# A decoder layer on one core: the first feed-forward layer as seven block products of sums of blocks

## The chip, the cores and the metric

The kernel runs on one core of one Trainium2 chip. The metric is the device time of one launch in microseconds (us); lower is better. Three runs of the kernel before gave 1168.57, 1169.19 and 1167.16 us, median 1168.57 us.

## The reference, cut to what matters

One decoder layer for 512 prompt tokens and 64 sample tokens (8 sequences of 8), 576 columns in all, width 1024: a mixer of gated linear attention and latent attention, a cross-attention into 256 memory tokens, and the feed-forward sublayer, which is all that the change touches:

```python
D_MODEL = 1024
D_FF = 4 * D_MODEL

def ffn(h, lp):
    u = jnp.maximum(h @ lp['w_ff1'], 0)
    return (u * u) @ lp['w_ff2']

x = x + ffn(rms_norm(x, lp['g_ff']), lp)
```

Everything is float32 in the reference. The first layer takes 1024 features to 4096, the second takes 4096 back to 1024.

## The kernel before, in words

**Layout.** Activations lie transposed: features on the 128 partitions, the 576 tokens as columns. `xT` holds x in KD = 8 tiles of 128 features. A matmul has a 128x128 block of weights as the stationary side and 288 columns (HALF, half of the tokens, index c) as the moving side; it adds into one of eight PSUM banks. Weights arrive in 512 KB tiles (128 output features by 1024 input features, or by 1024 hidden features for the second layer) in a ring of SLOTS = 8 buffers, `ring`. SP issues the loads in order, each when the slot's last contents have been split.

**Three terms.** Each float32 operand is split into a high part (rounded to the fp32r type) and a low part (what is left). A product is high x high, high x low, low x high (TERMS), so three matmuls for each block and half. The split weights lie in `wr`, those of h = x times the gain g_ff in `hr`, those of the squared hidden values in `ur`. The division by the norm is not done on h: the second layer's result is multiplied by `r_ff` = 1/(mean square + eps), which is enough because u is squared and relu keeps the factor.

**The stretch before.** The cross-attention's output projection (`xo`, matmuls L1372) makes 8 output tiles, each of two halves of 12 matmuls. Banks turn, and the last half (7, 1) lies in bank 0. DVE adds each half to `xT` (L2377, `add_half`) and frees its bank; behind each pair of additions it does the low part of the tile of h before it (L2430, `low_part`), for tiles 5 and 6 the low part of a weight tile too (L2440). ACT makes the high part (L1848) and the square of x (L1851); POOL adds the squares up in `acc` (L2820, `add_squares`).

**The feed-forward.** 64 weight tiles in two halves of the hidden features. In each half 16 tiles of the first layer (`split_tile`, L1388): 48 matmuls, 8 blocks x 3 terms x 2 halves of the columns, into two banks, and then 8 output tiles of the second layer, two weight tiles each. These are loops on every engine (`Fori`), each pass with 8 tiles. For each weight tile DVE makes the high part (L2597) and the low part (L2599); `wr` has SPLITS = 2 places. For each hidden tile ACT does the relu of both halves (L1860, L1863), the square (L1868) and its high part (L1870), and DVE the low part (L2609). For each output tile DVE multiplies a half by `r_ff` (L2628) and adds it to `xT` (L2631). After the first 16 hidden tiles PE sums `acc` over the partitions (L1404, key `ms_ff`, banks 4 and 5), and DVE adds eps (L2644) and takes the reciprocal (L2645), once for each half. The next matmuls, of output tiles 0 and 1, use banks 0 to 3. POOL has no work in the feed-forward after the squares. At the end PE turns `xT` back into rows (L1423).

**Order and waits.** Each engine runs its own queue in order. `filled`/`full` and `freed`/`reopen` are the semaphores of a bank: PE fills it and the reader waits, the reader frees it and PE waits before it starts a new sum there. `make_plan` gives each sum its bank. `w_high` and `w_split` count the split weights, `h_high` and `h_low` the parts of h, `u_high` and `u_low` the parts of the hidden values.

## Time and profile before

| | before |
|---|---|
| median of three runs | 1168.57 us |
| the profiled execution, its own time | 1168.92 us |
| its span, first to last instruction | 1167.1 us |
| PE busy (matmul) | 1132.3 us, 97% |
| PEld, weight loads | 1025.2 us, 88% |
| DVE busy | 649.9 us, 56% |
| ACT busy | 380.8 us, 33% |
| POOL busy | 313.0 us, 27% |
| mean granted TensorE clock | 0.992 of full speed |
| moved by DMA | 114.21 MB, mean 98 GB/s |

The span is the time that the trace covers; the execution's own time is 1.8 us longer. Busy is the share of the span in which an engine has an instruction in work; matmuls are pipelined, so the mean of one (296 ns) is longer than the pace at which they follow each other. The pace is the busy time of a group by the number in it.

### The profile page before, as it was taken

To read this page: it belongs to the slowest core of one execution; us is meant where nothing else is said; L and a number is where in the kernel's file an instruction comes from. 1 tells how busy PE (TensorE), PEld (TensorE's weight loads), DVE (VectorE), ACT (ScalarE), POOL (GpSimd) and SP (SyncE) were. 2 spreads that over 40 slices of the span, in tenths; PEclk is the share of its full clock that TensorE was granted. 3 is DMA by queue.
4 is the path that set the end of the run, shared out by engine and by line. 5 is a ranking of instruction groups with operands and counts; after the bars stand their busy time and mean duration, and the time that the engine had idled before them with its cause. 6 is when DMAs were issued, how large, how long until landed. Compare 5 with 4: busy or idle time off the path is not lost.

```text
span 1167.1 us, 22516 instructions
## 1 busy us (share of the span) xinstructions
PE 1132.3 (97%) x8288; PEld 1025.2 (88%) x8288; DVE 649.9 (56%) x1100; ACT 380.8 (33%) x872; POOL 313.0 (27%) x180
## 2 busy tenths in 40 slices
PE   7999999999999999999989989999999999999997
PEld 4799897577899999999869956999999999999996
DVE  0649653677566667766657566534354444444443
ACT  4331114455555445545502263423300013330001
POOL 0116224450277676876612201200000000000000
PEclk9999998999999999999999999999999999999999
DMA  9422102041454444454115240322223222222102
GB/s 339 175 91 91 59 1 64 1 133 68 122 158 120 122 127 122 135 143 126 40 41 212 91 162 20 109 91 73 90 73 91 75 87 86 77 90 73 55 0 81
DMA packets 61603, 114.21 MB, mean 98 GB/s; under 512 B 6577, under 2 KB 41554, under 8 KB 61458
## 3 DMA queue, kind: packets, MB, share of 16 engines
q1 hardware_dynamic: 60946, 111.33, 30.0%
q0 software_dynamic: 576, 1.84, 0.5%
q8 instruction: 45, 0.74, 0.3%
q14 instruction: 36, 0.29, 0.1%
HBM read 107.90 MB, written 5.25 MB: 97 GB/s over the span
## 4 chain that ended last, share of the span: by engine, by line
PE 88%; DVE 5%; POOL 2%; ACT 1%; DMA 1%; issue 1%; SPq 1%; POOLq 0%; DVEq 0%; ACTq 0%
PE bank L1388 35%; PE bank L1161 5%; PE bank L1230 5%; PE bank L1163 5%; PE bank L1162 5%; PE bank L811 4%; PE bank L829 4%; PE bank L773 3%; PE bank L1117 2%; POOL stat L2805 2%; PE bank L1372 2%; PE bank L991 2%; PE bank L1071 2%; PE bank L1169 1%; PE bank L977 1%; PE bank L1091 1%
## 5 line engine op out<-in xcount | busy, mean ns | idle before, releaser
L1388 PE MATMUL bank<-hr,wr 128*128 128x288 f32 x1536 | 205.2, 296 | 1.3 <-DVEq L2379 1.3
L1388 PEld LDWEIGHTS bank<-hr,wr 128*128 128x128 f32 x1536 | 204.9, 189 | 1.5 <-issue 1.5
L1388 PE MATMUL bank<-ur,wr 128*128 128x288 f32 x1536 | 205.3, 296 | 0.0
L1388 PEld LDWEIGHTS bank<-ur,wr 128*128 128x128 f32 x1536 | 205.0, 189 | 0.1
L2805 POOL TENSOR_TENSOR stat<-stat,cst 128x32 f32<-128x32 f32 x32 | 175.8, 5493 | 2.5
L2597 DVE CAST wr<-ring 128x1024 fp32r<-128x1024 f32 x62 | 43.0, 694 | 209.1 <-PE bank L1388 208.7
L1161 PE MATMUL bank<-wq_high,c_parts 128*128 128x288 f32 x512 | 156.8, 306 | 1.0 <-ACT mixT L1693 1.0
L1163 PE MATMUL bank<-wq_low,c_parts 128*128 128x288 f32 x512 | 151.7, 296 | 0.0
L1162 PE MATMUL bank<-wq_high,c_parts 128*128 128x288 f32 x512 | 150.3, 294 | 0.0
L2262 DVE TENSOR_REDUCE stat<-hT 128x8 f32<-128x512 f32 x128 | 86.7, 682 | 62.9 <-ACT hT L1711 61.0
L1161 PEld LDWEIGHTS bank<-wq_high,c_parts 128*128 128x128 f32 x512 | 96.1, 188 | 7.6 <-issue 7.1
L1162 PEld LDWEIGHTS bank<-wq_high,c_parts 128*128 128x128 f32 x512 | 96.4, 188 | 0.0
L1163 PEld LDWEIGHTS bank<-wq_low,c_parts 128*128 128x128 f32 x512 | 96.3, 188 | 0.0
L1860 ACT ACTIVATE hT<-bank 128x288 f32<-128x288 f32 x32 | 13.2, 412 | 236.2 <-PE bank L1388 236.2
L1711 ACT ACTIVATE hT<-bank 128x512 f32<-128x512 f32 x128 | 77.8, 608 | 0.3 <-DVE stat L2262 0.3
L2599 DVE TENSOR_TENSOR wr<-ring,wr 128x1024 fp32r<-128x1024 f32 x62 | 76.0, 1226 | 2.1
L1703 ACT COPY arena<-bank 128x64 f32<-128x64 f32 x128 | 27.2, 212 | 122.6 <-PE bank L1163 83.9
L2803 POOL TENSOR_TENSOR stat<-stat,cst 128x32 f32<-128x32 f32 x32 | 17.8, 557 | 82.4 <-DVE stat L2262 82.3
L811 PE MATMUL bank<-h_high,wz 128*128 128x288 f32 x176 | 38.3, 299 | 0.2 <-DVE ring_low L1948 0.2
L1877 ACT COPY hT<-bank 128x512 f32<-128x512 f32 (+1 forms) x5 | 2.9, 585 | 106.8 <-PE bank L1423 103.6
L811 PE MATMUL bank<-h_high,ring_low 128*128 128x288 f32 x176 | 37.5, 295 | 0.0
L811 PE MATMUL bank<-h_low,wz 128*128 128x288 f32 x176 | 37.5, 294 | 0.0
(421 smaller groups left out, 1964.4 us busy)
## 6 DMA issues: line engine op xcount, KB each, us to landing
ring<-in_ring_w_dram SPq DMA_DIRECT2D x106, 512.0 KB, 3.6
arena<-in_page_rows_dram SPq DMA_DIRECT2D x128, 144.0 KB, 2.2
hT<-in_ckv_t_dram SPq DMA_DIRECT2D x64, 128.0 KB, 2.1
arena<-in_ckv_t_dram SPq DMA_DIRECT2D x64, 128.0 KB, 2.1
arena<-in_mk_t_dram SPq DMA_DIRECT2D x8, 512.0 KB, 5.6
arena<-in_cache_mv_dram SPq DMA_DIRECT2D x8, 512.0 KB, 8.3
mixT<-in_x_dram SPq DMA_DIRECT2D x1, 2048.0 KB, 13.1
out_dram<-hT SPq DMA_DIRECT2D x4, 512.0 KB, 3.2
```

What stands on the lines that cost most here:

```text
L811: ins = mm(outs[c][:, 0:HALF], w_part(ew, tile)[:, k * P:(k + 1) * P], h_part(eh, k)[:, c * HALF:(c + 1) * HALF], start=(k == 0 and n == 0 ...
L829: ins = mm(outs[t][0:m, 0:width], h_part(eh, k)[:, c0:c0 + m], w_part(ew, tile)[:, kk * width:(kk + 1) * width], start=(k == 0 and n == 0) ...
L1161: mm(o[:, 0:WQ - QH], c_parts[:, n % 2, 0, e, k, :], high, start=(k == 0), stop=False)
L1162: mm(o[:, 0:WQ - QH], c_parts[:, n % 2, 1, e, k, :], high, start=False, stop=False)
L1163: ins = mm(o[:, 0:WQ - QH], c_parts[:, n % 2, 0, e, k, :], low, start=False, stop=(k == KC - 1))
L1230: ins = mm(outs[c][:, 0:HALF], w[:, k * P:(k + 1) * P], src[ex][:, k, c * HALF:(c + 1) * HALF], start=(k == 0 and n == 0), stop=(k == KD - ...
L1388: ins = mm(outs[c][:, 0:HALF], w[:, ew, k, :], src[:, ex, k0 + k, c * HALF:(c + 1) * HALF], start=(start and k == 0 and n == 0), stop=(sto ...
L1711: A(sqs[:, j % 2, :].rearrange("p (e c) -> p e c", e=2), o[:, :, keys_at:keys_at + WQ - 2 * QH], ACT.Square).then_inc(S("kr_free"), 1)
L2262: V.tensor_reduce(stat[:, 64 + 32 * g + 8 * (j % 4):72 + 32 * g + 8 * (j % 4)], sqs[:, j % 2, :].rearrange("p (h c) -> p h c", h=MH), AX.X ...
L2597: V.tensor_copy(wr[:, j % SPLITS, 0, :], src).then_inc(S("w_high"), 1)
L2599: V.tensor_tensor(wr[:, j % SPLITS, 1, :], src, wr[:, j % SPLITS, 0, :], ALU.subtract).then_inc(S("w_split"), 1)
L2805: G.tensor_tensor(r, r, power.broadcast_to([P, 32]), ALU.pow).then_inc(S("r_pg"), 1)
```

## The change

The first layer is computed by groups of two weight tiles, which are a 2 x 2 matrix of blocks: A11 and A12 are the upper and the lower 512 input features of the first tile (its 128 output features), A21 and A22 those of the second. h is a 2 x 2 matrix too: the upper or lower 512 features by the left or right 288 columns. Eight block products (of 12 matmuls: 4 blocks of 128 x 3 terms) are replaced by seven, of sums of blocks (Winograd's form of Strassen's product). The first group, g = 0, is left plain (`plain`), since h is then still arriving; 15 groups remain.

- **Weights.** POOL makes S1 = A21 + A22, S2 = S1 - A11, S3 = A11 - A21 and S4 = S2 - A12 (`weight_sum`, 128x512 each). The seven operands, of 128x512, are split by ACT (high part, `high_of`) and DVE (low part, `low_of`) into `wr`, which has OPERANDS = 7 places. All 16 second-layer operands of a quarter go the same way.
- **h.** DVE makes the sums of h for the four blocks k = 0 to 3 (`column_sums`, four instructions of 128x288 each); ACT and POOL (DVE for the fourth) split them, 128x1152 each.
- **Products.** `group`: A11, S2, S1, A22, A12, S3, S4, each 12 matmuls into one bank (`product`); A12, S3 and S4 are added onto the banks of A11, S2 and S1 after these have been read. The groups use banks 0 to 3 and 4 to 7 in turn.
- **Outputs of a group.** ACT copies A11 and S1 out, DVE makes the four hidden halves by five additions or subtractions of 128x288 (`outputs_of`); then relu, square and split as before.
- **Quarters.** Four quarters of the hidden features in place of two halves: 8 first-layer tiles, then 8 output tiles of one weight tile each (`second`), so `xT` gets four additions for each half tile in place of two. In the first quarter `ms_ff` stands after 8 hidden tiles, in banks 2 and 3.
- **No loops.** The feed-forward is written out on every engine.

The diff, cut to its core:

```diff
+M_ORDER = ("A11", "S2", "S1", "A22", "A12", "S3", "S4")
+BANK_OF = {"A11": 0, "A12": 0, "S2": 1, "S3": 1, "S1": 2, "S4": 2, "A22": 3}
...
+        if q == 0:
             for c in range(2):
+                fill(("ms_ff", c), 2 + c)
+        for j in range(KD):
             for c in range(2):
+                fill(("f2", q, j, c), (2 * j + c) % 8)
...
+            def product(name, g, start=True):
+
+                m = FIRST["g", g] + M_ORDER.index(name)
+                o = reopen(pe, (name, g))
+                pe.wait_ge(S("w_split"), split_number(m))
+                for k in range(HK):
+                    for n, (ew, ex) in enumerate(TERMS):
+                        ins = mm(o[:, 0:HALF], wr[:, m % OPERANDS, ew, k * P:(k + 1) * P], hr[:, X_OF[name], ex, k, :],
+                                 start=(start and k == 0 and n == 0), stop=(k == HK - 1 and n == 2),
+                                 skip_group_check=True)
+                filled(ins, (name, g))
...
+                pe.wait_ge(S("u_low"), KD * (q + 1) - 2)
+                second(q, 0, 0, KD - 2)
+                second(q, 1, 0, KD - 2)
+                pe.wait_ge(S("u_low"), KD * (q + 1))
+                second(q, 0, KD - 2, KD)
+                second(q, 1, KD - 2, KD)
...
+            act.wait_ge(S("ff_step"), 4 * HK)
+            for x in ("S2", "S1", "S3"):
+                nc.scalar.copy(hr[:, X_OF[x], 0, :, :], hf[:, X_OF[x], 1, :, :]).then_inc(S("h_high"), 1)
...
+            def high_group(g):
+
+                m, k = FIRST["g", g] + OPERANDS, 2 * g % KD
+                o = full(act, ("A11", g))
+                freed(nc.scalar.copy(m1[:, g % 2, :], o[:, 0:HALF]), ("A11", g))
+                high_of(m)
+                high_of(m + 1)
+                o = full(act, ("S1", g))
+                if g > 1:
+                    read(act, ("A22", g - 1))
+                freed(nc.scalar.copy(m5, o[:, 0:HALF]), ("S1", g))
+                high_of(m + 2)
+                high_of(m + 3)
+                o = full(act, ("A12", g))
+                act.wait_ge(S("u_low"), 2 * g)
+                freed(A(u_sb[:, 0, 0, :], o[:, 0:HALF], ACT.Relu), ("A12", g))
+                high_of(m + 4)
+                high_of(m + 5)
+                read(act, ("A22", g))
+                A(u_sb[:, 1, :, :], u_sb[:, 1, :, :], ACT.Relu).then_inc(S("u"), 1)
+                act.wait_ge(S("u"), 4 * g - 1)
+                A(u_sb[:, 1, :, :], u_sb[:, 1, :, :], ACT.Square).then_inc(S("u"), 1)
...
             def low_part_behind(j):
                 if j:
                     low_part(j - 1)
                 if j in (2, 4):
                     late_low(LATE_XO + 1 + j // 2)
+                if j > HK:
+                    column_sums(j - HK - 1)
                 if j in (5, 6):
+                    low_of(FIRST_OP + 2 * (j - 5))
+                    low_of(FIRST_OP + 2 * (j - 5) + 1)
...
+            def outputs_of(g):
+
+                m = FIRST["g", g] + OPERANDS
+                m1_g = m1[:, g % 2, :]
+                low_of(m)
+                o = full(dve, ("S2", g))
+                read(dve, ("A11", g))
+                freed(V.tensor_tensor(u2, m1_g, o[:, 0:HALF], ALU.add), ("S2", g))
+                for n in range(1, 5):
+                    low_of(m + n)
+                o = full(dve, ("S3", g))
+                read(dve, ("S2", g))
+                freed(V.tensor_tensor(m1_g, m1_g, o[:, 0:HALF], ALU.add), ("S3", g))
...
+                V.tensor_tensor(u_sb[:, 1, 1, :], m1_g, m5, ALU.subtract)
+                o = full(dve, ("A22", g))
+                freed(V.tensor_tensor(u_sb[:, 1, 0, :], m1_g, o[:, 0:HALF], ALU.add), ("A22", g))
+                low_of(m + 5)
+                o = full(dve, ("S4", g))
+                freed(V.tensor_tensor(u_sb[:, 0, 1, :], u2, o[:, 0:HALF], ALU.subtract), ("S4", g))
+                hidden_low(2 * g + 1, 1, 2 * g + 1)
+                hidden_low(2 * g, 0, 2 * g + 2)
+                low_of(m + 6)
...
+            def weight_sum(g, name, a, b, op, behind=None):
+
+                n = SUMS.index(name)
+                if behind is not None:
+                    pool.wait_ge(S("acc"), sum_number(g, SUMS.index(behind)))
+                if g > 1:
+                    pool.wait_ge(S("w_split"), split_number(FIRST["g", g - 1] + M_ORDER.index(name)))
+                G.tensor_tensor(sums_sb[:, n, :], a, b, op).then_inc(S("acc"), 1)
```

**What moves on DVE ahead of the feed-forward.** The two rows L2377 below are the last additions to `xT`, of tile 7; the second frees bank 0, the first bank of the feed-forward. Before:

```order
L2377 TENSOR_TENSOR xT<-xT,bank6 128x288 [waits x_cross,bank_full6]
L2430 SCALAR_TENSOR_TENSOR hr<-xT,gn,hr 128x576 [waits x_cross,h_high]
L2440 TENSOR_TENSOR wr<-ring,wr 128x1024 [waits w_high]
L2377 TENSOR_TENSOR xT<-xT,bank6 128x288 [waits bank_full7]
L2377 TENSOR_TENSOR xT<-xT,bank0 128x288 [waits x_cross,bank_full0]
L2430 SCALAR_TENSOR_TENSOR hr<-xT,gn,hr 128x576 [waits x_cross,h_high]
L2430 SCALAR_TENSOR_TENSOR hr<-xT,gn,hr 128x576 [waits h_high]
```

Now (L2571 is the addition, L2624 the low part of h, L2639 to L2647 `column_sums`, L2630 `low_of`):

```order
L2571 TENSOR_TENSOR xT<-xT,bank6 128x288 [waits x_cross,bank_full6]
L2624 SCALAR_TENSOR_TENSOR hr<-xT,gn,hr 128x2x288 [waits x_cross,h_high]
L2639 SCALAR_TENSOR_TENSOR hf<-xT,gn,arena 128x288 [waits h_high]
L2642 SCALAR_TENSOR_TENSOR hf<-xT,gn,hf 128x288 [waits ff_step]
L2644 SCALAR_TENSOR_TENSOR hf<-xT,gn,arena 128x288
L2647 SCALAR_TENSOR_TENSOR arena<-xT,gn,hf 128x288 [waits ff_step]
L2630 TENSOR_TENSOR wr<-ring,wr 128x512 [waits w_high] x2
L2571 TENSOR_TENSOR xT<-xT,bank6 128x288 [waits bank_full7]
L2571 TENSOR_TENSOR xT<-xT,bank0 128x288 [waits x_cross,bank_full0]
```

Four instructions stand between two pairs of additions that were not there; this happens behind tiles 5 and 6, and twice more behind tile 7.

**What moves on PE around `ms_ff`.** Before, the sums over the partitions go to banks 4 and 5 (L1404), and the output tiles behind them start in banks 0 to 3. Now, at the end of the first quarter (L1482 `product`, L1534 `ms_ff`, L1516 `second`):

```order
L1482 MATMUL bank6<-hr,wr 128x288 x11
L1534 MATMUL bank2<-rstd,cst 128x288 [waits bank_free2,acc]
L1534 MATMUL bank2<-rstd,cst 128x288 [waits bank_free3]
L1516 MATMUL bank0<-ur,wr 128x288 [waits bank_free1,w_split,bank_free0,u_low]
L1516 MATMUL bank0<-ur,wr 128x288 x23
L1516 MATMUL bank0<-ur,wr 128x288 [waits w_split]
L1516 MATMUL bank0<-ur,wr 128x288 x11
L1516 MATMUL bank2<-ur,wr 128x288 [waits w_split,bank_free3,bank_free2]
```

The names give the even bank of a pair. Only 36 matmuls stand between the sums and the next use of banks 2 and 3.

**What DVE has in its queue there.** The end of group 3 and what frees banks 2 and 3 (L2835 to L2849 `outputs_of`, L2814 `hidden_low`, L2860 and L2861 eps and reciprocal):

```order
L2846 TENSOR_TENSOR hT<-hT,bank6 128x288 [waits bank_full7]
L2630 TENSOR_TENSOR wr<-ring,wr 128x512 [waits w_high]
L2849 TENSOR_TENSOR hT<-hT,bank6 128x288 [waits bank_full6]
L2814 TENSOR_TENSOR ur<-hT,ur 128x576 [waits u_high] x2
L2630 TENSOR_TENSOR wr<-ring,wr 128x512 [waits w_high]
L2860 TENSOR_SCALAR bank2<-bank2 128x288 [waits bank_full2]
L2861 RECIPROCAL rstd<-bank2 128x288 [waits dve_step]
L2860 TENSOR_SCALAR bank2<-bank2 128x288 [waits bank_full3]
L2861 RECIPROCAL rstd<-bank2 128x288 [waits dve_step]
```

The reciprocals stand behind the group's two low parts of the hidden values, which wait for ACT.

## Rows read from the trace of the kernel before

**Rows 1.** The page: busy time; then the chain that ended last

```profile
PE 1132.3 (97%) x8288; PEld 1025.2 (88%) x8288; DVE 649.9 (56%) x1100; ACT 380.8 (33%) x872; POOL 313.0 (27%) x180
...
PE bank L1388 35%; PE bank L1161 5%; PE bank L1230 5%; PE bank L1163 5%; PE bank L1162 5%; PE bank L811 4%; PE bank L829 4%; PE bank L773 3%; PE bank L1117 2%; POOL stat L2805 2%; PE bank L1372 2%; PE bank L991 2%; PE bank L1071 2%; PE bank L1169 1%; PE bank L977 1%; PE bank L1091 1%
```

**Rows 2.** Groups by line and form, feed-forward: busy us, mean ns | idle before

```profile
L1388 PE MATMUL bank<-ur,wr 128*128 128x288 f32 x1536 | 205.3, 296 | 0.0
L1388 PE MATMUL bank<-hr,wr 128*128 128x288 f32 x1536 | 205.2, 296 | 1.3 <-DVEq L2379 1.3
L2609 DVE TENSOR_TENSOR ur<-hT,ur 128x576 f32 x32 | 24.3, 758 | 13.4 <-ACT ur L1870 13.4
L1868 ACT ACTIVATE hT<-hT 128x576 f32<-128x576 f32 x32 | 22.0, 687 | 3.0
L1870 ACT CAST ur<-hT 128x576 f32 x32 | 21.6, 675 | 3.9
L2628 DVE TENSOR_TENSOR bank<-bank,rstd 128x288 f32<-128x288 f32 x32 | 14.7, 459 | 8.9 <-PE bank L1388 8.9
L1860 ACT ACTIVATE hT<-bank 128x288 f32<-128x288 f32 x32 | 13.2, 412 | 236.2 <-PE bank L1388 236.2
```

**Rows 3.** Groups of other stages, for sizes that the feed-forward lacks

```profile
L1665 ACT CAST c_parts<-arena 128x512 fp32r<-128x512 f32 x32 | 19.9, 621 | 1.3 <-DMA arena<-in_page_rows_dram 1.3
L1746 ACT CAST mix_high<-mixT 128x1152 fp32r<-128x1152 f32 x3 | 3.4, 1171 | 0.0
L2502 DVE TENSOR_TENSOR hT<-hT,stat 128x512 f32<-128x512 f32 x4 | 2.8, 692 | 0.1
L2370 DVE TENSOR_TENSOR mix_low<-mixT,mix_high 128x1152 fp32r<-128x1152 f32 x3 | 4.0, 1352 | 0.2 <-DVE mix_low L2421 0.2
L2781 POOL TENSOR_TENSOR wq_low<-w_kvb,wq_high 128x512 fp32r<-128x512 f32 x2 | 2.5, 1266 | 0.2
L2712 POOL TENSOR_TENSOR mixT<-arena,mixT 128x1152 f32<-128x1152 f32 x1 | 3.1, 3143 | 10.0 <-ACT mixT L1512 10.0
```

**Rows 4.** Timeline of DVE into the feed-forward: start us, us

```profile
735.17 1.04 DVE L2377 TENSOR_TENSOR xT<-xT,bank 128x288 f32<-128x288 f32 x2
736.36 0.82 DVE L2430 SCALAR_TENSOR_TENSOR hr<-xT,gn,hr 128x576 fp32r<-128x576 f32 x1
737.10 1.22 DVE L2440 TENSOR_TENSOR wr<-ring,wr 128x1024 fp32r<-128x1024 f32 x1
738.23 1.05 DVE L2377 TENSOR_TENSOR xT<-xT,bank 128x288 f32<-128x288 f32 x2
739.43 1.25 DVE L2430 SCALAR_TENSOR_TENSOR hr<-xT,gn,hr 128x576 fp32r<-128x576 f32 x1
740.60 1.21 DVE L2440 TENSOR_TENSOR wr<-ring,wr 128x1024 fp32r<-128x1024 f32 x1
741.74 1.04 DVE L2377 TENSOR_TENSOR xT<-xT,bank 128x288 f32<-128x288 f32 x2
```

**Rows 5.** Timeline of PE there: last matmuls of `xo`, first of the feed-forward

```profile
741.24 0.29 PE L1372 MATMUL bank<-xo_high,ring_low 128*128 128x288 f32 x1
741.37 0.29 PE L1372 MATMUL bank<-xo_high,wo_high 128*128 128x288 f32 x1
741.50 0.29 PE L1372 MATMUL bank<-xo_low,wo_high 128*128 128x288 f32 x1
741.63 0.29 PE L1372 MATMUL bank<-xo_high,ring_low 128*128 128x288 f32 x1
743.18 2.08 PE L1388 MATMUL bank<-hr,wr 128*128 128x288 f32 x14 [1.26 <-DVEq L2379]
```

**Rows 6.** Timeline of POOL in the same stretch

```profile
738.63 1.44 POOL L2820 TENSOR_TENSOR rstd<-rstd,hT 128x576 f32<-128x576 f32 x1 [2.09 <-ACT hT L1851]
740.74 2.33 POOL L2820 TENSOR_TENSOR rstd<-rstd,hT 128x576 f32<-128x576 f32 x1 [0.68 <-ACT hT L1851]
```

**Rows 7.** Timeline of DVE around `ms_ff`

```profile
848.77 0.46 DVE L2644 TENSOR_SCALAR bank<-bank 128x288 f32<-128x288 f32 x1
...
851.61 1.96 DVE L2645 RECIPROCAL rstd<-bank 128x288 f32<-128x288 f32 x1
```

**Rows 8.** PE in two stretches: length, busy us (matmuls), granted clock, DMA share, GB/s

```profile
700.00:717.00 17.00, 15.57 (x86) 0.97 0.00 1
1160.00:1167.10 7.10, 0.38 (x4) 0.86 0.68 245
```

More of the change, by code:

```diff
@@ L446, in build @@
         acc = r_ff = rstd[:, :]
-        ACC_FF = 2 * (KD - 1) + XH
         pcxT = view(arena, 17920, XH, 2, TP)
@@ L1375, in _, with plain @@
                     filled(ins, ("xo", j, c))
[L1379 to L1384 removed]
+            def plain(j):
+                outs = [reopen(pe, ("plain", j, c)) for c in range(2)]
+                for k in range(KD):
+                    m = FIRST["g", 0] + 2 * j + k // HK
+                    if k % HK == 0:
+                        pe.wait_ge(S("w_split"), split_number(m))
+                    if j == 0:
@@ new lines, in group @@
+            def group(g):
+                product("A11", g)
+                if g == 1:
+                    pe.wait_ge(S("acc"), COLUMN_LOW[0])
+                product("S2", g)
+                if g == 1:
+                    pe.wait_ge(S("acc"), COLUMN_LOW[1])
+                product("S1", g)
+                if g == 1:
+                    pe.wait_ge(S("h_low"), KD + 1)
+                product("A22", g)
+                product("A12", g, start=False)
+                if g == 1:
+                    pe.wait_ge(S("acc"), COLUMN_LOW[2])
+                product("S3", g, start=False)
+                product("S4", g, start=False)
@@ L1401, in _ @@
+            for q in range(QUARTERS):
+                for g in range(GROUPS * q, GROUPS * (q + 1)):
+                    if g == 0:
+                        plain(0)
+                        plain(1)
+                    else:
+                        group(g)
+                if q == 0:
                     pe.wait_ge(S("acc"), ACC_FF)
@@ L2633, in _, with hidden_low @@
-            for _ in range(2):
-                dve.nop().then_inc(S("u_low"), 1)
             add_to_x("xo", "x_cross", in_turn, low_part_behind)
             low_part(KD - 1)
-            for half in range(2):
-                with dve.Fori(0, KF // 16) as i:
-                    hidden(half, i)
-                if half == 0:
-                    full(dve, ("ms_ff", 0))
+            column_sums(HK - 1)
+            def hidden_low(n, which, number):
+                dve.wait_ge(S("u_high"), number)
+                V.tensor_tensor(ur[:, 1, n % KD, :], u_sb[:, which, :, :].rearrange("p c n -> p (c n)"),
+                                ur[:, 0, n % KD, :], ALU.subtract).then_inc(S("u_low"), 1)
@@ L2642, in _ @@
+            for q in range(QUARTERS):
+                for g in range(max(1, GROUPS * q), GROUPS * (q + 1)):
+                    outputs_of(g)
+                if q == 0:
                     for c in range(2):
-                        o = bank[PLAN[("ms_ff", c)][0]]
+                        o = full(dve, ("ms_ff", c))
                         link(V.tensor_scalar(o[:, 0:HALF], o[:, 0:HALF], EPS, None, ALU.add))
```

366 lines of the change are left out of this document (231 added, 135 removed).

## The prediction

> **What bounds the kernel now.** I read the page first: PE is busy for 97% of the span, and the chain that ended last is PE nearly everywhere, 35% of it on L1388, the feed-forward [rows 1]. Then the groups of that stage: the two layers take 205.2 and 205.3 us for 1536 matmuls each, 133.6 ns per matmul, with 1.3 us of idle time in all [rows 2]. So a matmul left out there is worth 133.6 ns, as long as nobody makes PE wait. DVE, ACT and POOL wait for PE there now; the question is how near they come to it when each gets more work and PE less. For that I took durations of the same shapes from other stages [rows 3], and looked at two places in time: the way into the feed-forward [rows 4, 5, 6] and the reciprocals [rows 7].
>
> **Matmuls.** Two weight tiles cost 96 matmuls, 12.83 us. As a group they cost 7 x 12 = 84, 11.22 us. 15 groups save 180 matmuls: 180 x 0.1336 = **24.05 us**. The new products put twelve matmuls in a row into one bank. The `xo` matmuls of before do just that, and they start 0.13 us apart [rows 5], so I add nothing.
>
> For the pace the Trainium skill ("TensorE: Matmul & The Clock Gate", section "Wait — 56ns, not 53.3ns?") gives N / 2.4 GHz plus about 2.5 ns for bf16, an estimate of 122.5 ns at N = 288. By that the saving would be 22.1 us and the forecast 2 us higher; the rows have 133.6 ns, and they decide.
>
> **Into the feed-forward (a loss).** `plain(0)` starts in bank 0 and must wait for the last addition of `xo`, as before: PE's last `xo` matmul starts at 741.63, its next at 743.18, released by DVE [rows 5]. DVE is the engine behind time here: the pairs of additions start at 735.17, 738.23 and 741.74 [rows 4], while PE makes a pair in 24 matmuls, 3.2 us. Now two `column_sums` stand ahead of the last pair. Each has four instructions of 128x288; I take the 0.46 us of L2628 [rows 2] for each, which lie between about 0.37 apart back to back and 0.6 with a wait for the one before: 1.7 us for four, 3.4 us for two. POOL's additions stand in the way besides: one of them took 2.33 us in place of 1.44 beside a DVE instruction with two inputs in SBUF [rows 6], and L2430 took 1.25 in place of 0.82 beside another [rows 4]. I add 1.0 us, so the last pair ends 4.4 us later and PE starts at 747.6.
>
> Then group 1 needs all of the split sums of h. From the last addition (742.8 + 4.4 = 747.2): DVE does two low parts (0.8 each) and two `column_sums` (1.7 each), with one wait for POOL 6.0 us: 753.2. ACT's first 128x1152 cast 1.17 [rows 3]: 754.4. POOL then does the first low part, 3.14 at that size, and S1 and S2 of the weights, 1.27 each [rows 3]: 760.1. ACT stands behind them in its queue: casts of the two sums 1.2, two relus, a square and a cast of hidden tile 0, 2.3, two casts 1.2, two relus 0.7, the cast of the fourth sum of h 1.17: 766.7. DVE makes its low part in 1.35 [rows 3], but POOL may be in its third 3.14 us instruction: between 768.1 and 771.2, I take 769.6. There product A22 can start; four products of 1.60 us are left of the group: 776.0. Without any wait group 1 would have ended at 743.18 + 180 x 0.1336 = 767.2. The loss is **8.8 us**, between 6 and 11.7.
>
> **`ms_ff` (a loss).** Before, the output tiles in banks 0 to 3 (12.8 us) covered eps and the reciprocals, 848.77 to 853.57, 4.8 us [rows 7]. Now the next use of banks 2 and 3 comes 36 matmuls (4.8 us) and the two sums (0.5 us) after the group's end. DVE reaches the reciprocals only after the low parts of both hidden tiles, for which ACT does a relu, a square and a cast (0.69 + 0.69 + 0.68) and then 0.41 + 0.69 + 0.68 [rows 2]; with gaps and DVE's own 0.76 and 0.69 that is 5.9 us after the group's end, and with the reciprocals 10.7. PE waits 10.7 - 5.3 = 5.4; with a collision now and then **5.5 us**, between 4 and 7.
>
> **In the groups (a loss).** Work per group, against PE's 11.22 us: ACT seven casts of 128x512 at 0.62, four instructions of 128x288 at 0.41, five of 128x576 at 0.68, 9.4 us; DVE seven subtractions at 0.69, five at 0.46, two at 0.76, 8.7 us; POOL four at 1.27, 5.1 us [rows 2, 3]. Each fits alone. But they wait for each other. From ACT's copy of A11: copies, casts and the relu up to the cast of A12's weights 4.3 us, DVE's low part of it 0.7, three additions 1.4, ACT's three and three more 4.3, the last cast 0.6: a ring of 11.3 us, as long as PE's group. Its slack is what PE grants before it needs the banks of A11 and S2 again, about 1.2 us, once a quarter. And POOL's sums stop DVE: DVE's instructions with two SBUF inputs and POOL's together are 4.8 + 0.5 + 1.5 + 5.1 = 11.9 us in a group. With two POOL instructions on the ring it is 12.9 us, 1.7 above PE's. POOL has ring tiles to sum only in the first two groups of a quarter (the next quarter's tiles are not loaded yet), so I take half of it, 0.95 us, for the 8 middle groups, less 1.2 us of slack in three quarters: 7.6 - 3.6 = **4.0 us**, between 0 and 14 x 1.7 = 24.
>
> **Costed at nothing.** The splits of second-layer weights: 2 x 0.62 on ACT and 2 x 0.69 on DVE in 6.4 us of PE. The doubled additions to `xT`: four of 0.46 for each output tile, with the splits 3.2 of 6.4 us; if that cover went, each tile would cost what exceeds 6.4. The wait for the last hidden tiles of a quarter: `second` puts 72 matmuls, 9.6 us, ahead of it, and the low parts come 5.2 us after the group's end. The loads: the same 64 tiles of 512 KB, one in 5.6 us, some 94 GB/s; the kernel already moves more than that in its tail [rows 8]. The end: the last output tile has the same four DVE instructions behind it. The loops: none showed idle time on PE.
>
> **Sum.** -24.05 + 8.8 + 5.5 + 4.0 = -5.75 us. Against the execution's own 1168.92 that is 1163.2, and it stands 0.35 above the median: 1168.57 - 5.75 = **1162.8 us**.
>
> **The rivals.**
> *The covers hold.* DVE wins its collisions with POOL, and the ring of ACT and DVE stays within PE's group. For it: the durations have some overlap (the second of a pair starts before the first has ended), which shortens the ring. Against it: at the two ends the order of the queue alone makes the loss. -24.05 + 6 + 4.5 + 0.5 = -13: 1155.5 us.
>
> *The ring binds every group (slower).* Place: ACT's copy of A11 and DVE's `u2` addition, for which A12 and S3 wait. Price: 12.9 - 11.22 = 1.68 us in each of 14 groups, 23.5 us in place of 4: 1182.3 us. It needs POOL to be let in ahead of DVE each time, in every group. For it: in the rows a DVE instruction that met a POOL instruction did not share, it waited [rows 4, 6]. Against it: POOL has no sums to make in half of the groups. It decides from 24.05 - 14.3 = 9.75 us of waits, 0.70 us per group; at half its price the kernel takes 1171.
>
> The Trainium skill ("SBUF — State Buffer", section "Who interferes with whom") says that whichever of DVE and GpSimd issues first has the shared ports for its whole instruction and the other blocks. By that, 2.33 for 1.44 us agrees, and it speaks against this change: every weight sum can hold up DVE for its full length.
>
> *The clock falls.* PE now idles for some 6 us before the feed-forward and 5.5 us at `ms_ff`. In the trace the granted clock was 0.97 in 17 us with 1.4 us of idle time, and 0.86 in the tail, where PE has next to nothing to do [rows 8]. If it fell to 1.2 GHz for as long as PE had waited, the matmuls behind would cost up to 2.9 us more at `ms_ff`, and up to 0.5 at the start, where group 1 waits anyway for A22: 1166.2 us, at the very edge of what counts as no change, where I count it. The Trainium skill ("TensorE: Matmul & The Clock Gate", Part 1) has it that idleness throttles the array to half its clock until it has been busy for a while; at the small gaps of this trace the clock hardly showed it.
>
> **How the numbers follow.** 0.2%, 2.3 us, is about what a measurement of this kernel can tell from no change. The forecast has 0.48, the covers 0.14, the clock 0.15, the binding ring 0.23. Forecast and covers are faster by over 0.2%: 0.62. The clock is within: 0.15. The ring is slower: 0.23. The range goes down a little below the covers, to 1154, and up to 1176, which takes in the ring at up to two thirds of its price and leaves out about 0.15 above.
>
> **What would show it.** The first-layer matmuls should be 1356 in number and the second's 1536, at 133 ns each when nothing waits. PE should show a gap of 5 to 7 us before the first, a wait of some 2 to 5 us in group 1 whose releaser is the low part of the fourth sum of h, and one of 5 to 6 us at bank 2 released by the reciprocal. DVE and POOL instructions should be longer than alone in the first two groups of a quarter, and PE's waits in later groups should lie at A12 and S3. It would be wrong if PE went through the sums without the gap at `ms_ff`, or if groups of the last quarters took more than 12 us each, which is the ring.

## The result, and the profile after

The changed kernel takes 1171.62 us (median of 22 runs, 1167.13 to 1174.56), the kernel before 1168.36 us in 22 runs on the same chips. The ratio is 1.0024, with a 95% interval of 1.0013 to 1.0035: slower, by some 2.8 us, about as much as a measurement can tell (0.2%). The forecast was 1162.8. The time lies within its range, and the direction is wrong. The profiled execution took 1168.68 us, its span 1166.9; it is one of the quicker ones, so the trace is compared by stretches and not by its whole time.

The page, busy time:

```profile
PE 1113.3 (95%) x8108; PEld 1006.6 (86%) x8108; DVE 743.1 (64%) x1303; ACT 489.2 (42%) x1066; POOL 410.0 (35%) x243
```

PE is busy for 19 us less than in [rows 1], so the matmuls did go. The span did not shrink with them. The groups of the feed-forward on PE (line, form, count, busy us and mean ns, idle time before and what ended it) show where part of it went:

```profile
L1516 PE MATMUL bank<-ur,wr 128*128 128x288 f32 x1536 | 207.1, 297 | 5.8 <-issue 5.8
L1482 PE MATMUL bank<-hr,wr 128*128 128x288 f32 x1260 | 172.0, 298 | 8.0 <-DVE hr L2823 6.9 <-ACT hT L2029 0.9 <-DVE wr L2630 0.3
L1470 PE MATMUL bank<-hr,wr 128*128 128x288 f32 x96 | 15.1, 325 | 6.8 <-DVEq L2573 6.8
```

1260 and 96 are the 1356 first-layer matmuls. The idle time is 20.6 us against 1.3 in [rows 2], and the busy time is longer than the count explains: 15.1 us for 96 matmuls is 157 ns each, not 133.6. The timeline of PE (start, us, then the row, then the idle time before it) puts each in its place:

```profile
746.15 15.09 PE L1470 MATMUL bank<-hr,wr 128*128 128x288 f32 x96 [6.80 <-DVEq L2573]
761.08 1.76 PE L1482 MATMUL bank<-hr,wr 128*128 128x288 f32 x12
763.11 3.52 PE L1482 MATMUL bank<-hr,wr 128*128 128x288 f32 x24 [0.28 <-DVE wr L2630]
773.53 31.08 PE L1482 MATMUL bank<-hr,wr 128*128 128x288 f32 x216 [6.90 <-DVE hr L2823]
...
816.19 47.91 PE L1516 MATMUL bank<-ur,wr 128*128 128x288 f32 x348 [5.82 <-issue]
863.94 28.95 PE L1482 MATMUL bank<-hr,wr 128*128 128x288 f32 x216
893.18 16.27 PE L1482 MATMUL bank<-hr,wr 128*128 128x288 f32 x120 [0.29 <-ACT hT L2029]
909.30 51.35 PE L1516 MATMUL bank<-ur,wr 128*128 128x288 f32 x384
```

Three gaps, all in the first quarter: before the feed-forward, at A22 of group 1, at `ms_ff`. The quarters behind have one wait of 0.28 or 0.29 us each. And the same 216 matmuls take 31.08 us behind the second gap and 28.95 in the next quarter. The stretches of PE tell why (length, busy us and count of PE and PEld, DVE, ACT, POOL, then the granted clock, the DMA share and GB/s):

```profile
746.15:752.00 5.85, 5.85 (x28) 5.85 (x29) 5.74 (x9) 1.27 (x2) 1.41 (x1) 0.60 0.23 86
752.00:765.00 13.00, 12.72 (x95) 12.45 (x94) 5.94 (x6) 8.86 (x15) 10.91 (x6) 1.00 0.00 0
773.53:780.00 6.47, 6.47 (x33) 6.47 (x34) 6.39 (x8) 1.74 (x4) 3.85 (x3) 0.64 0.51 162
816.19:822.00 5.81, 5.81 (x34) 5.81 (x35) 0.00 (x0) 0.00 (x0) 0.00 (x0) 0.75 0.01 3
822.00:830.00 8.00, 8.00 (x62) 8.00 (x61) 5.76 (x12) 2.29 (x4) 0.00 (x0) 1.00 0.19 68
```

Behind each gap the granted clock is 0.60, 0.64 and 0.75, means between the two levels of 1.2 GHz (0.5) and 2.4 GHz (1.00), and then it is 1.00 again. In 746.15 to 752.00 PE never rested and did 28 matmuls, 209 ns each.

The account runs from the start of the last `xo` matmul (741.63 before, 739.05 after) to the first turning matmul at the end (1155.82, 1155.59). I call this **the stretch**: what lies ahead of it is the same code, and the last `xo` matmul started anywhere from 738.9 to 745.4 us in the traces of the changed kernel and its variants. It is 414.19 us before and 416.54 after, 2.35 more. By the starts in the timeline, against 133.6 ns a matmul:

- matmuls left out, 180 x 0.1336: -24.05;
- last `xo` matmul to the first of the feed-forward, 7.10 in place of 1.55: +5.55;
- plain group, 14.93 for 12.83: +2.10, clock;
- group 1 to the end of the quarter's first layer, 761.08 to 804.45 for 252 matmuls (33.67 us): +9.70, of it 7.18 waits, 2.06 slow matmuls behind A22 (30.92 us for 216, 28.86 at full pace), and 0.46 in the matmuls just before the two waits, whose ends lie behind the pace;
- the second layer of the first quarter with `ms_ff`, 805.21 to 863.94, 58.73 us for 384 matmuls that later take 51.19 (909.30 to 960.49): +7.54, of it 5.82 the wait, 1.36 slow matmuls behind it (47.75 us for 348, 46.39 at the later pace), and the rest before it;
- the later quarters, 45.36 for 336 matmuls (44.89): three times 0.47, +1.41.

The sum is +2.25, beside the measured 2.35 for these two traces.

What makes the second gap shows in DVE's timeline ahead of A22, one instruction a line, POOL's beside it, and ACT's cast of the fourth sum of h:

```profile
760.46 2.51 DVE L2630 TENSOR_TENSOR wr<-hT,wr 128x512 fp32r<-128x512 f32 x1 [3.21 <-ACT wr L1983]
762.89 1.77 DVE L2630 TENSOR_TENSOR wr<-hT,wr 128x512 fp32r<-128x512 f32 x1
764.59 1.84 DVE L2814 TENSOR_TENSOR ur<-hT,ur 128x576 fp32r<-128x576 f32 x1
766.35 3.12 DVE L2630 TENSOR_TENSOR wr<-ring,wr 128x512 fp32r<-128x512 f32 x1
769.40 1.75 DVE L2630 TENSOR_TENSOR wr<-ring,wr 128x512 fp32r<-128x512 f32 x1
771.07 2.41 DVE L2823 TENSOR_TENSOR hr<-arena,hr 128x1152 fp32r<-128x1152 f32 x1
```

```profile
759.73 2.68 POOL L3052 TENSOR_TENSOR hr<-hf,hr 128x1152 fp32r<-128x1152 f32 x1
762.37 1.75 POOL L3062 TENSOR_TENSOR hT<-ring 128x512 f32<-128x512 f32 x1
764.08 1.74 POOL L3062 TENSOR_TENSOR hT<-hT,ring 128x512 f32<-128x512 f32 x1
765.78 3.15 POOL L3052 TENSOR_TENSOR hr<-hf,hr 128x1152 fp32r<-128x1152 f32 x1
768.89 1.70 POOL L3062 TENSOR_TENSOR hT<-ring 128x512 f32<-128x512 f32 x1
770.67 1.59 POOL L3062 TENSOR_TENSOR hT<-hT,ring 128x512 f32<-128x512 f32 x1
```

```profile
764.58 1.15 ACT L2016 CAST hr<-arena 128x1152 fp32r<-128x1152 f32 x1
```

DVE has six instructions from 760.46 to 773.48 and POOL six from 759.73 to 772.26. Alone DVE's six would take 4 x 0.69 + 0.76 + 1.35 = 4.9 us [rows 2, 3]; they took 13.0, with no idle time in between. The two engines take turns, one instruction each: five of POOL's end at 762.4, 764.1, 765.8, 768.9 and 770.6, and 0.55 to 0.6 us behind each of them one of DVE's ends; the sixth of DVE's, the longer one, ends 1.2 us behind POOL's last. It is so in the rest of the trace: of 171 low parts of weights on DVE from 740 us on, 32 took 1.4 us or more, and within each of the 32 lies the end of exactly one POOL instruction. ACT's cast of the fourth sum of h ended at 765.73, and DVE's low part of it at 773.48.

### The profile page after: what moved, and what is told of

It is laid out like the page before. It is cut to its first block, busy times and chain, and to the rows that moved or that the text cites. A ratio compares the mean times of both kernels' runs of the same rounds, so it can differ in the third digit from the quotient of the medians.

```text
span 1166.9 us, 22259 instructions
## 1 busy us (share of the span) xinstructions
PE 1113.3 (95%) x8108; PEld 1006.6 (86%) x8108; DVE 743.1 (64%) x1303; ACT 489.2 (42%) x1066; POOL 410.0 (35%) x243
## 4 chain that ended last, share of the span: by engine, by line
PE 76%; DVE 9%; POOL 5%; ACT 4%; issue 3%; DMA 1%; POOLq 0%; SPq 0%; DVEq 0%; ACTq 0%
PE bank L1516 17%; PE bank L1482 9%; PE bank L891 6%; PE bank L1310 5%; PE bank L1241 4%; PE bank L909 4%; POOL stat L3025 4%; PE bank L1243 4%; PE bank L1242 4%; PE bank L1197 3%; PE bank L853 2%; DVE wr L2630 2%; PE bank L1071 2%; PE bank L1151 2%; PE bank L1452 1%
## 5 line engine op out<-in xcount | busy, mean ns | idle before, releaser
L1516 PE MATMUL bank<-ur,wr 128*128 128x288 f32 x1536 | 207.1, 297 | 5.8 <-issue 5.8
L1516 PEld LDWEIGHTS bank<-ur,wr 128*128 128x128 f32 x1536 | 206.3, 190 | 6.1 <-issue 6.0
L1482 PE MATMUL bank<-hr,wr 128*128 128x288 f32 x1260 | 172.0, 298 | 8.0 <-DVE hr L2823 6.9
L1482 PEld LDWEIGHTS bank<-hr,wr 128*128 128x128 f32 x1260 | 170.4, 190 | 9.3 <-DVE hr L2823 7.1
L1983 ACT CAST wr<-ring 128x512 fp32r<-128x512 f32 x113 | 66.8, 619 | 127.6 <-PE bank L1516 117.4
L3062 POOL TENSOR_TENSOR hT<-ring 128x512 f32<-128x512 f32 x30 | 44.1, 1472 | 209.7 <-DVE wr L2630 157.7
L2630 DVE TENSOR_TENSOR wr<-ring,wr 128x512 fp32r<-128x512 f32 x113 | 97.0, 887 | 4.8 <-ACT wr L1983 4.5
L2868 DVE TENSOR_TENSOR bank<-bank,rstd 128x288 f32<-128x288 f32 x64 | 29.6, 462 | 100.7 <-PE bank L1516 100.7
L3062 POOL TENSOR_TENSOR hT<-hT,ring 128x512 f32<-128x512 f32 x30 | 47.4, 1581 | 25.5 <-DVE wr L2630 24.3
L1983 ACT CAST wr<-hT 128x512 fp32r<-128x512 f32 x60 | 36.5, 620 | 47.4 <-PE bank L1516 31.6
L2630 DVE TENSOR_TENSOR wr<-hT,wr 128x512 fp32r<-128x512 f32 x60 | 50.5, 867 | 3.2 <-ACT wr L1983 3.2
L2814 DVE TENSOR_TENSOR ur<-hT,ur 128x576 fp32r<-128x576 f32 x32 | 27.8, 869 | 33.3 <-ACT ur L2048 18.2
```

The costliest lines, as they stand in the source:

```text
L1482: ins = mm(o[:, 0:HALF], wr[:, m % OPERANDS, ew, k * P:(k + 1) * P], hr[:, X_OF[name], ex, k, :], start=(start and k == 0 and n == 0), sto ...
L1516: ins = mm(bank[PLAN["f2", q, j, c][0]][:, 0:HALF], wr[:, m % OPERANDS, ew, k % HK * P:(k % HK + 1) * P], ur[:, eu, k, c * HALF:(c + 1) * ...
L1983: nc.scalar.copy(wr[:, m % OPERANDS, 0, :], source(m)).then_inc(S("w_high"), 1)
L2630: V.tensor_tensor(wr[:, m % OPERANDS, 1, :], source(m), wr[:, m % OPERANDS, 0, :], ALU.subtract).then_inc(S("w_split"), 1)
L3062: G.tensor_tensor(sums_sb[:, n, :], a, b, op).then_inc(S("acc"), 1)
```

## The experiments

Each kernel is the changed one with the edit shown. The stretch is read from its profiled execution, the ratio is against the kernel before.

**1. Other banks for `ms_ff`.**

```diff
-                fill(("ms_ff", c), 2 + c)
+                fill(("ms_ff", c), 4 + c)
```

> The two sums of ms_ff go to banks 4 and 5, as before the change, in place of 2 and 3; all else is the changed kernel (1171.6 us median, ratio 1.0024 to the kernel before; its profiled execution 1168.68). Gaps theory: the wait of 5.8 us ahead of output tile 1 goes, because banks 4 and 5 are wanted only 12.8 us after the sums, and with it the stretch at a granted clock of 0.66 to 0.76 behind it, worth about 1.9 us: 7 to 8 us less, ratio to the kernel before 0.996 to 0.998. Rival (DVE is behind in any case, so the wait only moves to output tile 2): 0 to 2 us less.

1164.7 us, ratio 0.9966 (0.9951 to 0.9981). The stretch is 409.10, 7.44 less than the change's, where the account has 7.54 for this gap. PE's groups in it:

```profile
L1516 PE MATMUL bank<-ur,wr 128*128 128x288 f32 x1536 | 205.6, 296 | 0.0
L1482 PE MATMUL bank<-hr,wr 128*128 128x288 f32 x1260 | 171.9, 297 | 8.3 <-DVE hr L2823 6.9 <-ACT hT L2029 0.9 <-DVE wr L2630 0.5
```

As expected, the wait is gone, and with it 1.5 us of busy time in the same 1536 matmuls. One wait of 5.82 us cost 7.4. The page puts this wait down to "issue" and names no releaser; that it is the banks of `ms_ff` follows from this run, and from the second reciprocal, which ends at 816.09, 0.1 us before PE goes on. The other two gaps stayed as they were.

**2. The fourth sum's low part ahead in DVE's queue.** ACT's cast of it comes first, DVE does it ahead of weight operands 10 and 11 and of the first hidden tile. On DVE:

```diff
-            hidden_low(0, 0, 1)
+            dve.wait_ge(S("h_high"), 2 * KD + 4)
+            V.tensor_tensor(hr[:, 3, 1, :, :], t4, hr[:, 3, 0, :, :], ALU.subtract).then_inc(S("h_low"), 1)
             low_of(10)
             low_of(11)
-            dve.wait_ge(S("h_high"), 2 * KD + 4)
-            V.tensor_tensor(hr[:, 3, 1, :, :], t4, hr[:, 3, 0, :, :], ALU.subtract).then_inc(S("h_low"), 1)
+            hidden_low(0, 0, 1)
```

> Around groups 0 and 1, ACT casts the fourth sum of h as soon as the plain tiles are read, ahead of the square and cast of hidden tile 0, and DVE makes its low part ahead of the low parts of two weight operands and of hidden tile 0. Order theory: the wait of 6.9 us ahead of product A22 of group 1 falls to 1 to 3 us and the slow clock behind it goes too, worth about 2: 5 to 7 us less than the changed kernel. Lock rival (DVE is held up by POOL's three low parts and four sums at that place whatever the order, since both are served in turn): the low part of the weights of A22 or A12 comes as late as the sum did, and the gain is under 2 us.

1170.59 us, ratio 1.0015 (0.9998 to 1.0031), stretch 416.17, 0.4 less than the change's. PE's timeline in group 1:

```profile
766.31 3.52 PE L1482 MATMUL bank<-hr,wr 128*128 128x288 f32 x24 [0.46 <-DVE wr L2632]
773.40 4.95 PE L1482 MATMUL bank<-hr,wr 128*128 128x288 f32 x24 [3.57 <-DVE wr L2632]
780.70 27.35 PE L1482 MATMUL bank<-hr,wr 128*128 128x288 f32 x192 [2.35 <-issue]
```

Waits of 0.28 and 6.90 became three, 6.4 together. The order in the queue only chooses which product waits; DVE's time is what is short. The theory of the order, by which 5 to 7 us were to go, falls.

**3. PE kept busy in the three gaps**, with matmuls whose result nobody reads (50, 50 and 42).

```diff
+                for i in range(n):
...
+                    mm(o[:, 0:HALF], w, x, start=True, stop=True)
...
+                    keep_busy(50, ("xo", 7, 0))
```

> 142 matmuls that compute nothing are put into PE's three long waits (50 before group 0, 50 ahead of product A22 of group 1, 42 ahead of output tile 1), into banks that are free. The waits themselves stay. Clock theory: the granted clock stays at 1.00 in and after the gaps; group 0 takes 12.8 us in place of 14.9, but product A22 starts when it did, since it waits for the low part of the fourth sum; what is gained is the slow stretch behind A22 and behind ms_ff, 2.5 + 1.9 = 4.4 us less than the changed kernel. Rival (the matmuls behind the gaps are slow for a reason of their own, such as the loads of instructions or the fresh banks): the same stretches stay slow, 0 us less or a little more.

1169.63 us, ratio 1.0005 (0.9992 to 1.0019), stretch 415.24, 1.3 less than the change's. PE's timeline:

```profile
752.52 13.01 PE L1481 MATMUL bank<-hr,wr 128*128 128x288 f32 x96 [0.26 <-DVEq L2588]
769.44 4.96 PE L1493 MATMUL bank<-hr,wr 128*128 128x288 f32 x24 [2.32 <-DVE wr L2645]
```

The filler gave the plain group its full clock, 13.01 us for 15.09, and the second layer 205.8 for 207.1. So the slow matmuls come from the gaps. But 4.4 us were expected, and 1.3 came. The plain group's 2.1 us came back as a wait of 2.32 for DVE, behind which 24 matmuls again took 4.96 us (some 3.4 at full pace). PE was early at a place where DVE sets the time, so the clock lost in the plain group was mostly cover, and only the clock behind A22 and behind `ms_ff` can be on the path. The filler also ran over the event that it covered: A22 started 35.6 us after the last `xo` matmul, in the change 34.5. From A22 to the end of the stretch 2.4 us were gained, of the 3.4 that the account has there as slow matmuls: at A12 of group 2 PE now waited 0.79 us for ACT (L2044), where it had not before.

**4. Weight sums of one column.** POOL adds one column of each sum of weights in place of 512; the rest of the first layer's sums is left out.

```diff
-                G.tensor_tensor(sums_sb[:, n, :], a, b, op).then_inc(S("acc"), 1)
+                G.tensor_tensor(sums_sb[:, n, 0:1], a[:, 0:1], b[:, 0:1], op).then_inc(S("acc"), 1)
```

> POOL makes one column of each weight sum in place of 512, with the same semaphores: this leaves out the sums of the weights, so the first layer's output means nothing. Lock theory: DVE's subtractions of 128x512 return from 880 ns to 690, the wait ahead of A22 in group 1 falls from 6.9 to 2 to 4 us, the wait at ms_ff by 1 to 2 us (its last two DVE instructions before the reciprocals were 0.6 and 1.1 us longer than alone), and the small waits of 0.29 us in later groups go: 5 to 8 us less with the clock. Rival (POOL's part in it is small, the order of the queues makes the waits): under 2 us less.

1159.03 us, ratio 0.9915 (0.9884 to 0.9945), stretch 404.85, 11.7 less. PE's group of the first layer, and DVE's low parts of ring tiles (in the changed kernel 887 ns):

```profile
L1482 PE MATMUL bank<-hr,wr 128*128 128x288 f32 x1260 | 168.9, 295 | 1.8 <-DVE hr L2823 1.8
...
L2630 DVE TENSOR_TENSOR wr<-ring,wr 128x512 fp32r<-128x512 f32 x113 | 78.6, 719 | 21.3 <-ACT wr L1983 21.1
```

That is more than the 5 to 8 us expected. POOL's additions cost nothing on PE themselves, and half of the change's gain: with them gone the wait at A22 fell from 6.9 to 1.8, the three ring waits vanished, and the wait at `ms_ff` fell from 5.82 to 4.12. DVE's instructions are back near the 0.69 us of [rows 3].

**5. The low parts of h's sums on DVE.** The three 128x1152 instructions of POOL go to DVE's queue, as POOL held DVE for them anyway.

```diff
+            for n, x in enumerate(("S2", "S1", "S3")):
+                dve.wait_ge(S("h_high"), 2 * KD + n + 1)
+                V.tensor_tensor(hr[:, X_OF[x], 1, :, :], hf[:, X_OF[x], 1, :, :], hr[:, X_OF[x], 0, :, :],
...
-                if g == 1:
-                    column_low(1, "S2")
```

> The low parts of the three other sums of h (128x1152 each) move from POOL to DVE, which stands idle there for 3.9 and 3.2 us; POOL then does the four weight sums of group 1 earlier. All else is the changed kernel. Lock theory (the wait at A22 of group 1 was DVE and POOL taking turns at each other's length): DVE's instructions of 4.20, 1.84, 4.79 and 2.41 us between 760 and 773 shrink to about 1.3, 0.8, 1.3 and 1.4; the low part of the fourth sum is ready some 7 us earlier, the wait of 6.9 us goes below 1.5 us and the slow clock behind it goes: the feed-forward, from the last matmul of xo to the first of the end, takes 405.5 to 408 us in place of 416.5, and the median is 8 to 10 us below 1171.6. Rival (queue order: ACT's casts are what is late): DVE waits for ACT instead, and 0 to 3 us are gained.

1168.46 us, ratio 0.9992 (0.9976 to 1.0007), stretch 410.85, 5.7 less than the change's. PE's timeline in group 1:

```profile
764.82 5.02 PE L1482 MATMUL bank<-hr,wr 128*128 128x288 f32 x36 [0.75 <-DVE wr L2630]
771.42 3.46 PE L1482 MATMUL bank<-hr,wr 128*128 128x288 f32 x24 [1.58 <-DVE hr L2827]
775.41 9.82 PE L1482 MATMUL bank<-hr,wr 128*128 128x288 f32 x72 [0.53 <-issue]
```

DVE got more work and PE waits less: 2.9 us in group 1 for 7.2. DVE does such a part in 1.35 us [rows 3], and POOL takes 2.7 to 3.2. Of the 5.7 us, 0.6 is the start, which was 5.87 us here and also when the unedited kernel ran again (experiment 10), so 5.1 are the edit's; 8.5 to 11 were expected. The time moved by less: the ratio fell from 1.0024 to 0.9992, 3.7 us, good to some 2. One reason shows behind the stretch: the turning matmuls at the end took 6.22 us in place of 4.56, at a granted clock of 0.75. Why, no run shows.

**6. Both, 1 and 5.**

> The edit of e5 together with that of e1 (ms_ff in banks 4 and 5). If the two waits are independent, the gains add: 7.4 us for the banks and 8 to 10 for the low parts, feed-forward 398 to 400.5 us, ratio to the kernel before 0.986 to 0.989. Rival (the ring of ACT and DVE then binds in the groups): 3 us or more are lost again in waits at A12 and S3.

1160.27 us, ratio 0.9924 (0.9898 to 0.995), stretch 403.61: 12.93 less than the change's, where the two alone gave 7.44 and 5.69, 13.13. The gaps are separate. The turning matmuls again took 6.22 us.

**7. The start gap too.** On top of 6 the plain group starts in banks 2 and 3, and all `column_sums` stand behind the last low part of h.

```diff
-            fill(("plain", j, c), 2 * j + c)
+            fill(("plain", j, c), 2 * (1 - j) + c)
...
-                if j > HK:
-                    column_sums(j - HK - 1)
```

> The edit of e6, and the way into the feed-forward: plain(0) uses banks 2 and 3, which are free early, and all four column_sums stand behind the last low part of h. The wait of 6.8 us ahead of group 0 should fall to 1 to 3 us (PE starts within 0.5 us and then waits for the parts of the last two tiles of h), and with it the granted clock of 0.64 to 0.70 behind it goes. If DVE's and POOL's chain to group 1 keeps up, 5 to 7 us less than e6, ratio 0.981 to 0.984. If that chain is what sets group 1's end, the gain is only the clock's, 0 to 2 us.

1160.12 us, ratio 0.9921 (0.9896 to 0.9946), stretch 403.90: nothing beside 6. PE's timeline, and DVE's:

```profile
765.11 10.02 PE L1482 MATMUL bank<-hr,wr 128*128 128x288 f32 x60 [9.64 <-DVE wr L2630]
```

```profile
749.68 1.55 DVE L2644 SCALAR_TENSOR_TENSOR hf<-xT,gn,arena 128x288 f32<-128x288 f32 x1
...
755.05 0.51 DVE L2647 SCALAR_TENSOR_TENSOR arena<-xT,gn,hf 128x288 f32<-128x288 f32 x1
```

The gap of 5.6 us at the start is gone, the plain group took 12.9 us, and behind it is one of 9.64. The work for group 1 was not done sooner; PE only reached it sooner: it started 22.7 us after the last `xo` matmul, against 22.4 in experiment 6. POOL's last addition of squares and its four weight sums of group 1, which now ran beside the first `column_sums`, stretched five of DVE's sixteen instructions from 0.51 to some 1.5 us.

**8. Every weight sum twice**, from group 2 on.

```diff
+                if g > 1:
+                    G.tensor_tensor(sums_sb[:, n, :], a, b, op).then_inc(S("wq"), 1)
...
```

> POOL makes each weight sum of groups 2 to 15 twice (56 instructions more, the result is the same); all else is the changed kernel. This measures the slack of the ring in the groups. If the ring has slack, as the waits of 0.29 us a quarter say: the small waits grow to at most 1 us a quarter, 0 to 3 us in all. If the ring was close to binding, as forecast: each POOL instruction more costs about its 1.3 us in the groups where POOL sums, 5 to 15 us.

1194.7 us, ratio 1.0218 (1.0191 to 1.0246), stretch 438.85, 22.3 more than the change's. What PE waits for in it (us in total, times, longest):

```profile
PE bank L1482 <- ACT hT L2029: 11.6, 10, 3.1
PE bank L1482 <- DVE hr L2823: 6.9, 1, 6.9
...
PE bank L1482 <- DVE hT L2835: 5.7, 6, 1.0
```

The ring binds, and where the prediction put it: ACT's copy of A11, for which A12 waits, and DVE's `u2` addition, for which S3 waits. The cost is above the 5 to 15 us expected. In the change itself the ring costs 0.9 us of waits; how much more POOL work it would bear before it decides, no run shows.

**9. Two plain groups.** On top of 7, group 1 is computed as eight products like group 0, so that the sums of h and of weights have 25.7 us of PE in place of 12.8; POOL begins on weights behind the last `column_sums`. Two orders change with it: the low parts of three weight operands go ahead of the `column_sums` on DVE, and the fourth sum's cast and low part come only at the last plain tile. This gives up one group's saving, 12 matmuls, 1.6 us.

```diff
+PLAIN = 2
...
-            if g == 0:
+            if g < PLAIN:
...
+            pool.wait_ge(S("ff_step"), 4 * HK)
+            for g in range(PLAIN, QUARTERS * GROUPS):
```

> The edit of e7 (DVE makes the low parts of the sums of h, ms_ff in banks 4 and 5, plain(0) in banks 2 and 3, column_sums behind the last low part), and a second plain group: groups 0 and 1 are done with eight products each, so 14 groups save 12 matmuls in place of 15, 1.6 us more of matmuls; POOL starts its sums behind the column_sums. The chain of DVE and ACT up to the low part of the fourth sum then has 25.7 us of PE's work as cover in place of 12.8. If that chain is all that stands in the way in e7 (its wait of 9.6 us and the clock of 0.59 behind it), both go: feed-forward 403.9 - 9.6 - 1.9 - 0.5 + 1.6 = 393 to 395 us from the last matmul of xo to the first of the end, ratio to the kernel before 0.981 to 0.984. If each saved wait comes back as one further on, as from e6 to e7, the ratio stays at 0.990 to 0.993.

1152.84 us, ratio 0.9849 (0.9827 to 0.9871); the stretch is 744.37 to 1139.75, 395.38 us, 18.8 less than before. PE's groups:

```profile
L1517 PE MATMUL bank<-ur,wr 128*128 128x288 f32 x1536 | 205.6, 296 | 0.0
L1483 PE MATMUL bank<-hr,wr 128*128 128x288 f32 x1176 | 158.3, 295 | 0.9 <-ACT hT L2034 0.9
L1471 PE MATMUL bank<-hr,wr 128*128 128x288 f32 x192 | 27.4, 306 | 1.8 <-DVE wr L2635 1.8
```

168 matmuls are worth 22.4 us, and 18.8 of them arrive. That is about what was expected (393 to 395 us). One wait of 1.8 us is left, with slow matmuls behind it, and the three of 0.3 us in the later quarters. This is the fastest version measured, 1.5% under the kernel before.

**10. The changed kernel again**, on the chip of the others.

> The changed kernel as it is, profiled once more, to see how much of its time is the same in another execution. If the cost is in the feed-forward's fixed waits, the stretch from the last matmul of xo to the first of the end is again 416 to 417 us (414.2 in the kernel before), with gaps of 6.8, 6.9 and 5.8 us, whatever the stages ahead of it do. If the clock behind the gaps varies from one execution to the next, the stretch moves by 1 to 3 us with the same gaps.

1170.01 us, ratio 1.0007 (0.9987 to 1.0028), stretch 415.95, 0.6 less than in the first trace; the gaps are 5.58, 6.85 and 5.22. The costs repeat; the split differs, with a shorter gap at the start and slower matmuls behind it (15.72 us for the plain group, 15.09 in the first trace). The ratio by itself would not tell the change from none; with the 22 runs it is slower by 0.24%.

## Why the prediction was wrong, point by point

The time lies in the range by luck: the upper end, 1176, was there for a ring that binds every group, and it is not the ring that cost the time.

**Matmuls: right.** 3072 became 2892, at 133.3 ns each where nothing waits (909.30 to 960.49 is 51.19 us for 384), and a row of twelve into one bank added nothing.

**The start: the mechanism right, the size near.** PE was to start its first feed-forward matmul 5.97 us after the last `xo` one, with a loss of 4.4; it was 7.10, a loss of 5.55, and 5.87 when the kernel ran again. The difference, 1.23 us, is who went first when DVE met POOL's addition of squares ahead of tile 6: two low parts of weights took 2.52 us in the first trace; in the second they took 1.29 and POOL waited for both.

**Into the feed-forward: the step that failed.** The place and the releaser (the low part of the fourth sum) were right, the size was not. The prediction had a loss of 8.8 us up to the end of group 1, between 6 and 11.7. Measured by the starts: 5.55 + 2.10 + 9.70 = 17.35. In the working it is this sentence that broke: "DVE makes its low part in 1.35, but POOL may be in its third 3.14 us instruction". It allows for one wait. By the timeline above, ACT's cast ended 26.7 us after the last `xo` matmul, 1.6 later than worked out; the low part then came 7.7 us later, in place of 2.9, because two low parts of weights stood ahead of it in DVE's queue and each of the three had to let a POOL instruction pass. Two low parts of weights in DVE's queue were not in the working at all. The prediction knew the exclusion, priced it inside the ring at DVE's and POOL's sum, and did not do the same on this path. Experiments 2, 4 and 5 show the cause: another order moves the wait, and fewer or shorter POOL instructions take most of it away (1.8 and 2.9 us are left). The stated bounds were off as well: 768.1 and 771.2 for the low part give a loss of 7.3 to 10.4 us, not 6 to 11.7.

**`ms_ff`: the wait right, its size partly luck, its price low.** 5.5 us was forecast, 5.82 measured. DVE's timeline there has the reciprocal at 1.96 us as before [rows 7], and two low parts that met POOL:

```profile
808.31 1.38 DVE L2814 TENSOR_TENSOR ur<-hT,ur 128x576 fp32r<-128x576 f32 x1 [1.01 <-ACT ur L2056]
809.61 1.76 DVE L2630 TENSOR_TENSOR wr<-ring,wr 128x512 fp32r<-128x512 f32 x1
...
814.13 1.96 DVE L2861 RECIPROCAL rstd<-bank 128x288 f32<-128x288 f32 x1
```

They took 0.76 and 0.68 us in experiment 4, where POOL's sums are gone: 1.70 us less together, which is just what the wait fell by (5.82 to 4.12). So without POOL the wait is 4.1, where the working has 5.4 for it and 0.1 for collisions; two errors nearly cancelled. The matmuls before and behind the wait added the other 1.7.

**The clock: a rival that should have been a term.** The prediction took 2.9 us at most at `ms_ff` and 0.5 at the start, gave it 0.15, and left it out of the sum; the evidence was a stretch with small gaps [rows 8], and 5 us gaps were what the forecast itself had just put into the kernel. Three gaps were followed by 2.1, 2.1 and 1.4 us of slow matmuls, 5.5 together; without the first, PE would have waited for DVE in its place, so at most 3.4 are the clock's own, and the filler of experiment 3 won 2.4 of them. Experiment 1 shows the last, 3 the first and its cover. The Trainium skill ("TensorE: Matmul & The Clock Gate", Part 1) was cited for idleness that throttles the array until it has been busy a while; the granted clock of 0.50 to 0.75 behind each gap agrees.

**In the groups: the place right, the size too high.** 4.0 us was forecast, 1.41 measured. The ring's waits are at A12, released by ACT L2029, 0.29 us once in each later quarter. The working has two slips here: half of 1.7 is 0.85 and not 0.95, which would have made 3.2 us of the 4.0, and the ring of 11.3 us with two POOL instructions of 1.27 is 13.8, not 12.9. With the POOL work doubled (experiment 8) the ring binds; the kernel then loses 5.6 us a quarter (22.3 / 4), not all of it on the ring.

**Covers hold: wrong** at all three places.

The sum was -24.05 + 8.8 + 5.5 + 4.0 = -5.75, and measured -24.05 + 17.35 + 7.54 + 1.41 = +2.25, 8.0 us more. Of these 8.0, 5.5 are slow matmuls, 0.8 the matmuls' ends before the waits, 4.3 waits beyond what was allowed, nearly all of them on the way to the end of group 1, and -2.6 the groups.

## What to carry to other kernels

Where a change takes work from a full engine and gives it to idle ones, the gain per unit is the easy part; look at the entries and exits of the stage, where the new work has no cover yet, and give the first steps the old form until it has (experiment 9). Where DVE and POOL both work on SBUF tensors, cost every DVE instruction on the path with one POOL instruction ahead of it, for as long as POOL has a queue. And when the forecast itself opens gaps of some 5 us on PE, put the slow matmuls behind each into the sum, unless PE is early there anyway.
